# All selection rounds between the attention's row maxima; x's second half turned inside the first weight unit; the first expert job's weights, flags and x parts moved or cut

## The reference, cut to what matters

```python
def dsa_branch(q, k, v, q_i, k_i, w_i, pos):              # the sparse one of the two attentions
    ...
    dots = jnp.einsum('bqhd,bsd->bqhs', qib, k_i)
    score = jnp.einsum('bqh,bqhs->bqs', wib, jax.nn.relu(dots))
    score = jnp.where(key_pos[None, :] <= q_pos[:, None], score, -jnp.inf)
    _, idx = lax.top_k(score, n_sel)                      # 64 keys of 256 for each query
    ...

def moe_ffn(x, w_router, w1, w3, w2):
    t = x.reshape(B * S, D)
    logits = (t @ w_router).astype(jnp.float32)
    top_val, top_idx = lax.top_k(logits, TOP_K)
    top_w = jax.nn.softmax(top_val, axis=-1)
    comb = jnp.sum(jax.nn.one_hot(top_idx, N_EXPERTS) * top_w[..., None], axis=1)
    for e in range(N_EXPERTS):
        y = y + comb[:, e:e + 1] * swiglu(t, w1[e], w3[e], w2[e])

for l in range(DEPTH):
    h = mixer_sublayer(x, ...)                            # x @ w_in is its first product
    x = layer_norm(ALPHA * x + h, ln1_g[l], ln1_b[l])
    f = swiglu(...) if l % 2 == 0 else moe_ffn(...)
    x = layer_norm(ALPHA * x + f, ln2_g[l], ln2_b[l])
```

## Time and profile before

| | before |
|---|---|
| median of three runs | 1624.46 us (1624.42 to 1627.68) |
| the profiled execution | 1625.77 us, span 1624.1 us |
| mean granted TensorE clock | 0.994 |
| TensorE matmul busy | 1591.0 us, 98% of the span |
| VectorE busy | 1293.2 us, 80% |
| ScalarE busy | 1024.6 us, 63% |
| GpSimd busy | 58.9 us, 4% |
| DMA | 453.13 MB, mean 279 GB/s |

### The profile page before, as it was taken

How to read it: one execution, slowest core, us unless ns; L and a number is a source line. 1 busy time by engine, 2 the same in 40 slices (tenths; PEclk the granted TensorE clock), 3 DMA queues, 4 the chain that set the end, 5 groups by cost and what they waited for, 6 DMA issues and landing times.

```text
span 1624.1 us, 19196 instructions
## 1 busy us (share of the span) xinstructions
PE 1591.0 (98%) x7629; PEld 1322.8 (81%) x7630; DVE 1293.2 (80%) x1302; ACT 1024.6 (63%) x947; POOL 58.9 (4%) x54
## 2 busy tenths in 40 slices
PE   8999999999999999999999999999999999999996
PEld 7888788888788788878888888888888888888885
DVE  6794675445788468899889888889888889888887
ACT  5655544343465645776777776777776777776773
POOL 0000000000000002000000100000100000100000
PEclk9999999999999999999999999999999999999998
DMA  9543366556453355999999999999999999999992
GB/s 326 181 140 117 105 219 208 184 184 201 135 176 130 104 181 178 361 358 324 368 372 363 362 377 328 366 378 365 370 373 327 366 375 360 373 374 328 370 372 85
DMA packets 230687, 453.13 MB, mean 279 GB/s; under 512 B 9920, under 2 KB 15552, under 8 KB 230592
## 3 DMA queue, kind: packets, MB, share of 16 engines
q1 hardware_dynamic: 228400, 447.60, 78.1%
q10 hardware_dynamic: 2192, 4.23, 0.7%
HBM read 450.75 MB, written 1.05 MB: 278 GB/s over the span
## 4 chain that ended last, share of the span: by engine, by line
PE 90%; DVE 7%; ACT 2%; issue 1%; DMA 0%; DVEq 0%; ACTq 0%
PE bank L1528 27%; PE bank L1530 27%; PE bank L1529 27%; PE bank L2003 3%; DVE split L425 2%; PE bank L1698 1%; ACT split L419 1%; PE bank L1916 1%; DVE split L441 1%; PE bank L1889 0%; PE bank L1890 0%; PE bank L1727 0%; PE bank L1726 0%; ACT split L436 0%; DVE x L1241 0%
## 5 line engine op out<-in xcount | busy, mean ns | idle before, releaser
L441 DVE TENSOR_TENSOR split<-raw,split 128x2048 fp32r<-128x2048 f32 x327 | 747.7, 2289 | 103.1 <-ACT split L436 101.9
L436 ACT CAST split<-raw 128x2048 fp32r<-128x2048 f32 x327 | 625.5, 1914 | 185.5 <-PE bank L1530 185.5
L1528 PE MATMUL bank<-split,xe_pair 128*128 128x512 f32 x784 | 310.0, 395 | 0.5 <-DVE split L441 0.5
L1530 PE MATMUL bank<-split,xe_pair 128*128 128x512 f32 x784 | 305.9, 390 | 0.0
L1529 PE MATMUL bank<-split,xe_pair 128*128 128x512 f32 x784 | 305.3, 389 | 0.0
L425 DVE TENSOR_TENSOR split<-raw,split 128x2048 fp32r<-128x2048 f32 (+3 forms) x96 | 208.3, 2174 | 111.3 <-ACT split L419 110.9
L419 ACT CAST split<-raw 128x2048 fp32r<-128x2048 f32 (+3 forms) x96 | 174.4, 1817 | 168.6 <-PE bank L1530 168.3
L1528 PE MATMUL bank<-split,xT 128*128 128x512 f32 (+2 forms) x544 | 217.8, 400 | 4.3 <-DVE split L425 2.4
L1530 PE MATMUL bank<-split,xT 128*128 128x512 f32 (+2 forms) x544 | 208.7, 384 | 0.0
L1529 PE MATMUL bank<-split,xT 128*128 128x512 f32 (+2 forms) x544 | 208.7, 384 | 0.0
L1528 PE MATMUL bank<-split,hT 128*128 128x512 f32 x488 | 190.6, 391 | 0.0
(11 more groups left out here) (248 smaller groups left out, 1604.1 us busy)
## 6 DMA issues: line engine op xcount, KB each, us to landing
raw<-moe_w_dram SPq DMA_DIRECT2D x330, 1024.0 KB, 6.1
raw<-w_in_dram SPq DMA_DIRECT2D x31, 1024.0 KB, 5.1
raw<-dense_w_dram SPq DMA_DIRECT2D x30, 1024.0 KB, 5.1
raw<-w_out_dram SPq DMA_DIRECT2D x8, 1024.0 KB, 5.1
early<-moe_w_dram SPq DMA_DIRECT2D x6, 1024.0 KB, 14.0
raw<-w_o_mla_dram SPq DMA_DIRECT2D x4, 1024.0 KB, 5.1
raw<-w_o_dsa_dram SPq DMA_DIRECT2D x4, 1024.0 KB, 5.4
raw<-w_in_dram SPq DMA_DIRECT2D x4, 912.0 KB, 5.2
```

The lines of the kernel that those rows point to most:

```text
L436: act.copy(split[:, n % SPLIT, HEAD, :], landing(n, j)[:, :]).then_inc(heads_made, 1)
L441: dve.tensor_tensor(split[:, n % SPLIT, REST, :], landing(n, j)[:, :], split[:, n % SPLIT, HEAD, :].bitcast(F32), ALU.subtract).then_inc(r ...
L1528: pe.matmul(out_, act_[REST], w[HEAD], start=first, stop=False)
L1530: return pe.matmul(out_, act_[HEAD], w[REST], start=False, stop=last)
```

## The change

In the start, `turn_half` for the second half of x moves on TensorE from between the two token tiles of the first unit to between the two halves of the first tile's products. Its two kept-warm calls there had a count of zero, so they issued nothing.

In the attention of both layers, rounds 1 and 2 of `best_keys` move from ahead of `maxima(0)` to behind `maxima(0)` and `maxima(1)`; rounds 3 to 7 each stand two heads later; the rest of unit 16 moves behind `maxima(0)`, that of unit 17 behind `maxima(1)`, and `selection` behind `maxima(7)`.

In the first expert job, the routing weights and flags move on VectorE from ahead of the job's fourth unit (counted from 0, unit 3) to behind the rest of unit 6; the split of x is made in four pieces of 512 channels in groups 1 to 4 (ScalarE in the first, VectorE in the second w2 unit); `y` is scaled in four pieces in groups 3 to 6. The gather of the next pair waits for all four pieces.

```diff
+        def piece_of_x(i):
+            return i // 2, slice(i % 2 * W, (i % 2 + 1) * W)
...
-                    if kind == "first" and (w, g, half) == ("w2", 2, 0):
+                    if kind == "first" and (w, half) == ("w2", 0) and 1 <= g <= 4:
+                        t, at = piece_of_x(g - 1)
                         act.wait_ge(rests_made, EARLY[0] + 1)
-                        act.copy(x_parts[HEAD][:, :, :], x[:, :, :]).then_inc(x_head_made, 1)
+                        act.copy(x_parts[HEAD][:, t, at], x[:, t, at]).then_inc(x_head_made, 1)
...
-            E = EXPERTS
-            dve.wait_ge(pos_mm, 2)
...
-            dve.sem_inc(routed, 1)
+            def weights_and_crowding():
+                E = EXPERTS
+                dve.wait_ge(pos_mm, 2)
...
+                dve.sem_inc(routed, 1)
...
-                    if kind == "first" and (w, g, half) == ("w2", 2, 1):
-                        dve.wait_ge(x_head_made, 1)
-                        dve.tensor_tensor(x_parts[REST][:, :, :], x[:, :, :], x_parts[HEAD][:, :, :].bitcast(F32), ALU.subtract).then_inc(x_rest_made, 1)
+                    if kind == "first" and (w, g, half) == ("w3", 0, 1):
+                        weights_and_crowding()
+                    if kind == "first" and (w, half) == ("w2", 1) and 1 <= g <= 4:
+                        t, at = piece_of_x(g - 1)
+                        dve.wait_ge(x_head_made, g)
+                        dve.tensor_tensor(x_parts[REST][:, t, at], x[:, t, at], x_parts[HEAD][:, t, at].bitcast(F32), ALU.subtract).then_inc(x_rest_made, 1)
+                    if kind == "first" and (w, half) == ("w3", 0) and g >= NG - 4:
+                        t, at = piece_of_x(g - (NG - 4))
+                        step(dve.tensor_scalar(y[:, t, at], x[:, t, at], ALPHA, None, ALU.mult))
...
-                if kind == "first":
-                    for t in range(T):
-                        step(dve.tensor_scalar(y[:, t, :], x[:, t, :], ALPHA, None, ALU.mult))
...
                 rest(15)
-                rest(16)
-                best_keys(range(1, 3))
...
                 for u in range(16):
                     maxima(u)
-                    if u == 0:
-                        rest(17)
-                    if u < 5:
-                        best_keys(range(3 + u, 4 + u))
+                    if u < 2:
+                        rest(16 + u)
+                    if u < 7:
+                        best_keys(range(1 + u, 2 + u))
                     if u == 4:
                         rest(18)
-                    if u == 6:
+                    if u == 7:
                         selection()
...
                     if (l, c, half) == (0, 0, 0) and i % 2 == 0:
+                        if (i, t) == (2, 0):
+                            pe.wait_ge(x_in2, 16)
+                            for tile in range(T):
+                                turn_half(0, tile, 1)
                         pe.wait_ge(rests_made if i else first_rest, 1)
...
                     if (l, m) == (0, 0):
-                        keep_warm(pe, t, 0 if t else 4)
-                        pe.wait_ge(x_in2 if t else x_in, 16)
-                        for tile in range(T):
-                            turn_half(0, tile, t)
-                        keep_warm(pe, t, 0 if t else 4)
+                        if t == 0:
+                            keep_warm(pe, 0, 4)
+                            pe.wait_ge(x_in, 16)
+                            for tile in range(T):
+                                turn_half(0, tile, 0)
+                            keep_warm(pe, 0, 4)
...
-                    pe.wait_ge(x_rest_made, 1)
+                    pe.wait_ge(x_rest_made, 2 * T)
```

More of the change, by code:

```diff
@@ L1046, in dve_experts @@
             make_rest(dve, FIRST + SPLIT - 1)
-            E = EXPERTS
-            dve.wait_ge(pos_mm, 2)
-            over, s1, s2, s4 = (flags[0:1, i * 16:(i + 1) * 16] for i in range(4))
-            step(dve.tensor_scalar(over[:, E:2 * E], bank[4][0:1, 0:E], float(CAP), None, ALU.is_gt))
-            dve.wait_ge(exp_done, 1)
-            step(dve.tensor_tensor(r_exp, r_exp, r_sel, ALU.mult))
-            step(dve.reduce_sum(r_one[:, :, 1:2], r_exp, AX_X))
-            step(dve.reciprocal(r_one[:, :, 2:3], r_one[:, :, 1:2]))
@@ L1057, in dve_experts @@
-            dve.tensor_tensor(r_comb, r_exp, r_one[:, :, 2:3].to_broadcast([P, T, EXPERTS]), ALU.mult).then_inc(placed, 1)
-            dve.wait_ge(placed, 1)
-            dve.tensor_copy(cur[:, 2:4], r_comb[:, :, 0:1].rearrange("p t n -> p (t n)")).then_inc(comb_put, 1)
-            for src, dst, by in ((over, s1, 1), (s1, s2, 2), (s2, s4, 4)):
-                step(dve.tensor_tensor(dst[:, E:2 * E], src[:, E:2 * E], src[:, E - by:2 * E - by], ALU.add))
-            step(dve.tensor_copy(jobs[0:1, 0:E], over[:, E:2 * E]))
```

16 lines of the change are left out of this document (14 added, 2 removed).

## The result

The changed kernel takes 1614.76 us, the median of four runs (1612.78 to 1615.03); the kernel before, run beside it, 1625.18 (1624.42 to 1627.68, four runs). The ratio is 0.9931, with a 95% interval of 0.9913 to 0.9948: 10.4 us faster. (The three runs known before the prediction had 1624.46; a fourth, beside the changed kernel, made it 1625.18.) The profiled execution took 1614.98 us, its span 1613.3.

A forecast was written before the change was run, and what follows sets the result against it. TensorE, busy 98% of the span, was taken as the bound, so only its waits and clock could give time. Start 3.2, attention 4.1 and first job 2.2 sum to 9.5 us: forecast 1615.0 us, range 1612.5 to 1619.5.

The forecast's parts named there:

- The start: Kernel start: x's transposes six matmuls earlier bring unit 1 forward 1.66 us, without the slow clock stretch; 3.2 us in all.
- at 10.62: Start: the time in us when the eight transposes of x's second half would begin, instead of 12.28.
- The clock: Start: the granted clock's fall to 0.50 for 3.40 us, after the wait at 16 us, would no longer come.
- Rival 1: Start or new wait: the clock falls anyway, 1.5 to 3 us less gain, 1617 us; chance 0.12.
- The attention: Both layers: the wait of `qk` for a row maximum goes in full, 2.06 us a layer, 4.1 in all.
- rival 5: Attention: the rounds become VectorE's bound, up to 1.44 us for each of seven rounds in two layers, 1639 us; chance 0.03.
- The first job: First expert job: old waits go (1.5, 1.3, 0.7 us), a new one at unit 7 costs 1.3; gain 2.2 us.
- Rival 3: First expert job: GpSimd's picks hold rests 7 and 8, up to four times 0.6 us, 1615.6 to 1617.4; chance 0.06.
- rival 2: Start: unit 1 lands 1.7 us later than its 0.17 us margin allows, losing 3.2 us, 1618.2; chance 0.08.
- rival 4: First expert job: the small instructions find room and no new wait comes, 1613.7 us; chance 0.08.
- rival 6: Later stretches: gains are given back; half of 9.5 us lost gives 1620, all about 1624; chance 0.13.

The follow-up runs named there:

- the start: The kernel before with only x's second half turned inside the first tile on TensorE: 1624.31 us, one run.
- the rounds: The kernel before with, in the attention, only the selection rounds and the selection moved: 1624.78 us, one run.
- the weights: The kernel before with, in the first expert job, only the twelve small instructions (weights and flags) moved behind the rest of unit 6: 1624.1 us.
- the pieces: The kernel before with, in the first expert job, only x's split and the scaling of y in pieces: 1623.39 us.
- both attention edits: The kernel before with only the attention's part of the change, rests and selection rounds both moved: 1618.61 us, one run.
- the rests: The kernel before with, in the attention, only the rests of units 16 and 17 moved behind row maxima 0 and 1: 1619.93 us, one run.
- the flags apart: The changed kernel with the weights left behind the rest of unit 6 and the flags moved into unit 9: 1613.21 us, five runs.

## Why the prediction came out right

The forecast was 1615.0, measured 1614.76 and again 1614.53. Such closeness is luck in part. The gain was forecast as 9.5 us and was 10.4 by the medians of one comparison and 10.8 by the spans of the profiles; the start gave less than its term, and a stretch of the clock that has no term in the sum gave 1.6.

- **The start, 3.2 us forecast, 2.5 seen.** The order of events was right but for the time of the clock's rise: transposes six matmuls earlier, unit 1 there in time, idle 0.85 (forecast 0.8), no slow stretch at 18. What failed is "at 10.62". It took the kernel before's clock for granted. In the profile of the changed kernel the first matmuls of the first unit still step by 0.43 us, those of 1.2 GHz, and the transposes come later:

```profile
9.70 0.63 PE L1536 MATMUL bank<-split,xT 128*128 128x512 f32 x1
10.12 0.63 PE L1537 MATMUL bank<-split,xT 128*128 128x512 f32 x1
...
11.36 1.04 PE L2015 MATMUL bank<-ident,x 128*128 128x128 f32 x8
```

  Unit 1 then comes at 17.34 instead of 16.6. The fourteen profiles sort by when the clock rose. Order is that of x's second half, old (between the token tiles) or new (in the first tile); the times are the start of unit 1 and of the first scores, in us:

```
clock rose at      order  profiles  unit 1            first scores      1.2 GHz at 18
about 8 to 9 us    old    4         18.17 to 18.26    101.00 to 101.17  in all 4
about 8 to 9 us    new    3         16.48 to 16.55    97.79 to 97.89    in none
10.2 to 10.4 us    old    2         18.45, 18.49      99.75, 99.83      in none
about 10.8 us      new    2         17.34, 17.36      98.68, 98.67      in none
13.2 to 14.6 us    new    3         18.42 to 18.58    99.79 to 99.90    in none
```

  With an early rise on both sides the start gives 1.6 to 1.8 us at unit 1 and 3.1 to 3.4 at the first scores: the 3.2 of the forecast, both terms. With a rise at 10 to 11 us it gives 1.1, since there the old order has no slow stretch to lose either. The kernel before was profiled with an early rise and the changed kernel with a later one, which is where 0.7 us went. The old order has no profile with a rise at 13 us or later, so what the move is worth there, and whether the new order makes such a rise more frequent (3 of 8 profiles, 0 of 6), stays open.
- **The clock, 1.5 us at the start.** Rival 1 did not come at 18: none of the eight profiles with the new order has a slow stretch there. The changed kernel's own profile proves little by it, since with a late rise the old order has none either; the three with an early rise, against four of four with the old order, show it. But the second half of it, a slow stretch elsewhere, is the rule and not the exception. Before has three of 3.4 us; the changed kernel had one (behind `oa` of layer 1) in one profile and none in the other, and the profile with none had the late rise at the start. The prediction counted the one at 18 and not the two others. The one behind the first attention was missing in the profile after, which is the 1.6 us in the account above and more than fills what the start lacked. No term of the forecast stands for it, so here the number was helped by luck. It is not plain chance of the run, though. In the five profiles of kernels that still wait for `mx` (before, the start, the rounds, the weights, the pieces) a stretch at 1.2 GHz follows `oa` in both layers, ten of ten. In the five without that wait and with the old end of the attention (the changed kernel twice, both attention edits, the rests, the flags apart) it follows in four places of ten. So the attention's edit seems to have made it rarer; why, and in which run it comes, no run here shows.
- **The attention, 4.1 us forecast, 2.15 and 2.12 seen.** Sum right, and the new times too (row maximum 1 forecast 2.0 us ahead of TensorE's need, and done at 104.78 against scores that began at 106.50, so 1.7). The cause was named wrongly. "VectorE's own list" and rival 5's "two rounds and a rest were crowded ahead of it" make the rounds the cause; by the halves done alone the rounds are worth 0.4 us a layer and the rests all of it, 2.16. The row that says so was in hand: VectorE idle 2.85 us for head 17. An engine that waits is not short of time; one instruction in its list stands too early.
- **The first job, 2.2 us forecast, 2.5 seen.** The wait at unit 3 went, the two behind the parts of x went, and the new one stands at unit 7, as forecast. Its size was off, 0.69 idle for 1.1 to 1.2. VectorE's side was forecast to 0.1 us (small instructions done at 651.3, less the lead of 8.30 with which the job began, is 643.0; rest 7 starts behind them, just at 642.96). TensorE came later than forecast, ready for unit 7 at 644.45 (0.23 behind the matmul of 644.22) for 644.2: since the job's start its lead had grown by 1.28, not by the 1.5 put down for the wait at unit 3. The delay was then 0.85, and idle time counted from a modelled end is 0.16 shorter, which the prediction itself says and left out in this size. VectorE there:

```profile
640.53 0.15 DVE L1057 TENSOR_SCALAR flags<-bank 1x8 f32<-1x8 f32 x1
...
642.96 4.50 DVE L441 TENSOR_TENSOR split<-raw,split 128x2048 fp32r<-128x2048 f32 x2
...
647.97 2.35 DVE L441 TENSOR_TENSOR split<-early,split 128x2048 fp32r<-128x2048 f32 x1
```

- **Rival 3, GpSimd's picks.** They ran from 642.06 beside these three rests:

```profile
642.06 6.36 POOL L579 TENSOR_SCALAR pair_pick<-slot_no,small 128x128 fp32r<-128x128 f32 x4 [0.22 <-POOL small L574]
```

  Four picks took 6.36 us where the shortest takes 0.6, while the rests took 2.25, 2.25 and 2.35. GpSimd's work took longer again, and the most that a rest may have lost is 0.1 us. The rule of the Trainium skill ("SBUF — State Buffer", "Who interferes with whom"), that whichever starts first blocks the other, shows here in one direction only: one pick took 4.6 us across the rests, while the last pick, from 647.82 for 0.60 us, began ahead of the rest of 647.97 and didn't hold it by the 0.45 us that they share (2.35 us, where the rests around it took 2.25 to 2.31). The times on GpSimd are rough, though.
- **Rivals 2, 4, 5 and 6** did not come: unit 1 was not held by its landing, a new wait is there, no row maximum is late, and the lead never shrinks between two of the marks above.

## What to carry to other kernels

Where an engine's list makes another wait, look at what stands just ahead of the urgent instruction, and whether the engine was busy or idle there. VectorE was idle for a head that was not ready: moving that one rest behind the next urgent instruction gave the whole wait back, 2.15 us a layer, and moving two rounds of work around it gave 0.4. ScalarE was busy with a head that nobody needed yet: moving it gave 1.1 us a layer. And a step that is moved earlier should be priced at both levels of the clock where it lands: here the same move was worth 3.1 to 3.4 us with an early rise on both sides and 1.1 with a later one.

## What the runs showed of the hardware

- At the start the matmuls run at 1.2 GHz until 8 to 15 us of the span, differently in each profile of nearly the same program, and the clock column of the windows shows 1.00 there; only the step of the matmuls (0.43 instead of 0.23 us for 512 columns) tells it. All slow stretches between the start and the last matmul are 3.4 us long. They followed idle times of 2.2 us (at 16 to 18 us), of 0.86 and 0.97 us with work between (the end of the attention), and of 1.43 and 0.52 us (behind it). After its last matmul TensorE shows 0.50 for the last 8 to 12 us of every profile, which costs nothing but lowers the mean granted clock.
- One such stretch cost 1.55 us behind the attention's end and 1.05 behind the turning of x.
- A late rise of the clock and a slow stretch can hide each other in the total: the changed kernel took 1614.98 us with unit 1 at 17.34 and one stretch, and 1614.52 with unit 1 at 18.42 and none.
- An extra 128x128 float32 matmul, identity by identity, counts as two in the records, about 0.12 us each; a transpose of the same size counts as one (eight of x in 1.03 us).
- Four GpSimd picks beside rests took 6.36 us, the longest of them 4.6, while the rests beside them took 2.25 to 2.35 us.
